# Experts in three chunks of 1024, 896 and 896 FF columns instead of six of 512 and 256

## What is computed

```python
def _moe(h, router_w, router_b, exp_gate, exp_up, exp_down):
    logits = (h @ router_w).astype(jnp.float32) + router_b.astype(jnp.float32)
    top_val, top_idx = lax.top_k(logits, TOP_K)
    wts = jax.nn.softmax(top_val, axis=-1)
    combine = jnp.sum(jax.nn.one_hot(top_idx, N_EXPERTS, dtype=jnp.float32) * wts[..., None], axis=-2)
    y = jnp.zeros_like(h)
    for e in range(N_EXPERTS):
        y = y + combine[..., e:e + 1] * _swiglu(h, exp_gate[e], exp_up[e], exp_down[e])
    return y

def _swiglu(h, w_gate, w_up, w_down):
    return (jax.nn.silu(h @ w_gate) * (h @ w_up)) @ w_down
```

## Time and profile before

| what | value |
| --- | --- |
| median of the runs | 1841.0 us |
| the profiled execution's own time | 1840.1 us |
| its span | 1838.2 us |
| TensorE busy | 1678.1 us, 91% |
| VectorE busy | 1247.9 us, 68% |
| ScalarE busy | 991.5 us, 54% |
| expert e0 (two tiles), first to last product | 912.5 to 1115.3 us of the span |
| experts e1 to e7 (one tile each) | 1115.3 to 1794.5 us |

### The profile page before, as it was taken

One profiled execution on the slowest core, in us unless ns is written; L12 is line 12 of the kernel. 1 busy time (PEld: TensorE's weight loads), 2 busy tenths in 40 slices (PEclk: granted clock), 3 DMA queues, 4 the chain that ended last, 5 costly groups with the idle time before them and its releaser, 6 DMA issues.

```text
span 1838.2 us, 20709 instructions
## 1 busy us (share of the span) xinstructions
PE 1678.1 (91%) x7867; PEld 1386.1 (75%) x7867; DVE 1247.9 (68%) x1518; ACT 991.5 (54%) x1322; POOL 88.7 (5%) x100
## 2 busy tenths in 40 slices
PE   6879989899999979998799998999999989999990
PEld 4767767788778758997687776878887878788780
DVE  5565356755453456766554456989988978998886
ACT  5753354343332342444443435778777767787770
POOL 0003300110000000000000000000000000000003
PEclk8989999999999989999799999999999999999995
DMA  8643235396454335655255557999999999999983
GB/s 310 203 138 116 69 130 165 99 316 247 140 177 138 106 100 168 199 183 183 96 183 180 163 186 269 373 363 376 378 375 370 376 333 356 370 379 375 378 320 114
DMA packets 205244, 436.59 MB, mean 238 GB/s; under 512 B 13391, under 2 KB 46778, under 8 KB 205114
## 3 DMA queue, kind: packets, MB, share of 16 engines
q1 hardware_dynamic: 195050, 398.20, 61.7%
q0 software_dynamic: 8368, 30.42, 4.9%
q10 hardware_dynamic: 1696, 6.29, 0.9%
HBM read 426.59 MB, written 20.86 MB: 243 GB/s over the span
## 4 chain that ended last, share of the span: by engine, by line
PE 73%; DVE 9%; DMA 7%; ACT 5%; issue 4%; POOL 1%; SPq 0%; ACTq 0%; DVEq 0%; POOLq 0%
PE ps L517 22%; PE ps L519 21%; PE ps L518 21%; DVE w_lo L436 5%; DMA raw<-in_exp_gate 3%; ACT w_hi L430 2%; DMA raw<-in_exp_up 2%; PE ps L1164 1%; PE ps L702 1%; PE ps L703 1%; ACT hf L1427 1%; DMA raw<-in_w_mod 1%; PE ps L931 1%; PE ps L730 1%; DVE prod_exp L2165 0%
## 5 line engine op out<-in xcount | busy, mean ns | idle before, releaser
L436 DVE TENSOR_TENSOR w_lo<-raw,w_hi 128x1024 fp32r<-128x1024 f32 (+1 forms) x760 | 893.5, 1217 | 247.3 <-ACT w_hi L430 240.6
L430 ACT CAST w_hi<-raw 128x1024 fp32r<-128x1024 f32 (+1 forms) x760 | 767.4, 1047 | 391.3 <-PE ps L519 269.7
L517 PE MATMUL ps<-w_hi,gT_hi 128*128 128x512 f32 x792 | 317.5, 401 | 19.3 <-DVE w_lo L436 9.2
L519 PE MATMUL ps<-w_hi,gT_lo 128*128 128x512 f32 x792 | 311.6, 393 | 0.0
L518 PE MATMUL ps<-w_lo,gT_hi 128*128 128x512 f32 x792 | 311.1, 393 | 0.0
L517 PE MATMUL ps<-w_hi,prodT_hi 128*128 128x512 f32 x528 | 211.5, 401 | 8.8 <-DVE prod_dense L2165 5.2
L519 PE MATMUL ps<-w_hi,prodT_lo 128*128 128x512 f32 x528 | 207.2, 392 | 0.0
L518 PE MATMUL ps<-w_lo,prodT_hi 128*128 128x512 f32 x528 | 206.8, 392 | 0.0
L517 PEld LDWEIGHTS ps<-w_hi,gT_hi 128*128 128x128 f32 x792 | 150.4, 190 | 53.6 <-issue 11.7
L519 PEld LDWEIGHTS ps<-w_hi,gT_lo 128*128 128x128 f32 x792 | 150.3, 190 | 32.4
L518 PEld LDWEIGHTS ps<-w_lo,gT_hi 128*128 128x128 f32 x792 | 150.5, 190 | 29.5
(11 more groups left out here) (357 smaller groups left out, 1843.7 us busy)
## 6 DMA issues: line engine op xcount, KB each, us to landing
raw<-in_exp_gate SPq DMA_DIRECT2D x176, 512.0 KB, 5.7
raw<-in_exp_up SPq DMA_DIRECT2D x176, 512.0 KB, 5.7
raw<-in_exp_down SPq DMA_DIRECT2D x176, 512.0 KB, 5.2
raw<-in_w_mod SPq DMA_DIRECT2D x96, 512.0 KB, 4.8
y_rows<-in_exp_up POOLq DMA_DIRECT2D x8, 1536.0 KB, 28.8
raw<-in_w_in_conv SPq DMA_DIRECT2D x24, 512.0 KB, 6.3
raw<-in_ffn_gate SPq DMA_DIRECT2D x22, 512.0 KB, 5.2
raw<-in_ffn_up SPq DMA_DIRECT2D x22, 512.0 KB, 5.9
```

The costliest lines, as they stand in the source:

```text
L430: nc.scalar.copy(w_hi[:, s, cols], raw[:, n % RAW, cols]).then_inc(sem("w_hi_ready"), 1)
L436: nc.vector.tensor_tensor(w_lo[:, s, cols], raw[:, n % RAW, cols], w_hi[:, s, cols].bitcast(F32), ALU.subtract).then_inc(sem("w_ready"), 1)
L517: nc.tensor.matmul(out, a[0], b[0], start=start, stop=False)
L519: return nc.tensor.matmul(out, a[1], b[0], start=False, stop=stop)
```

## The change

The experts get a list of their own, `EXP_ORDER`, of 36 units. Chunks are 1024, 896 and 896 FF columns. A gate or up unit holds two K blocks, each of the chunk's whole width, one DMA for each (rows of 4096 or 3584 bytes); a down unit holds two K blocks as before or, at the first of chunk 1 and the last of chunk 2, one. The list is gate 0, up 0, gate 1, down 0, up 1, gate 2, two units of down 1, up 2, two units of down 1, down 2, four units each where no count is given. With one tile, gate has banks 0 and 1, up 2 and 3, down 4 and 5. With more tiles, tile s has banks 2s and 2s + 1 for gate, up and down alike, and `banks_free` has TensorE wait, wherever the kind changes, until ScalarE or VectorE has read them; the down sums of an expert then go to `Y` in three parts (a copy and two additions) instead of two. Silu and the multiplication run once a chunk; the turning follows in four groups a chunk. The next expert's rows are asked for after unit 26 of 36 and turned after unit 33. The dense layer keeps its code.

```diff
+EXP_CHUNKS = [(0, 1024), (1024, 896), (1920, 896)]
+EXP_GROUPS = [(2, 2, 2, 2), (1, 2, 2, 2), (2, 2, 2, 1)]
+EXP_ORDER = [(kind, c, i) for kind, c, part in
+             (("gate", 0, range(4)), ("up", 0, range(4)), ("gate", 1, range(4)), ("down", 0, range(4)), ("up", 1, range(4)),
+              ("gate", 2, range(4)), ("down", 1, range(2)), ("up", 2, range(4)), ("down", 1, range(2, 4)),
+              ("down", 2, range(4))) for i in part]
+EXP_UNITS = len(EXP_ORDER)
+EXP_BLOCKS = FF // P
+GROUPS = 4 * len(EXP_CHUNKS)
+
+
+def exp_at(kind, c, i=3):
+    return EXP_ORDER.index((kind, c, i))
+
+
+TURN_AT = {exp_at("gate", c + 1, i): [4 * c + i] for c in (0, 1) for i in range(4)}
+TURN_AT |= {exp_at("down", 1, 2): [8, 9], exp_at("down", 1, 3): [10, 11]}
+ROWS_AT, TURN_ROWS_AT = exp_at("up", 2, 0), EXP_UNITS - 3
+
+
+def group_blocks(g):
+
+    sizes = EXP_GROUPS[g // 4]
+    return sum(sizes[:g % 4]), sizes[g % 4]
+
+
+def turns_at(u, tiles):
+
+    groups = TURN_AT.get(u, [])
+    if tiles > 1 and u == exp_at("down", 1, 2):
+        return []
+    return TURN_AT[u - 1] + groups if tiles > 1 and u == exp_at("down", 1, 3) else groups
...
+def flat_banks(ps, base, first, n):
+    return ps.rearrange("p b n -> p (b n)")[:, 512 * base + first:512 * base + first + n]
...
-        return ffn(w["exp_gate"][0][expert], w["exp_up"][0][expert], w["exp_down"][0][expert], n - U_MOE)
+        kind, c, i = EXP_ORDER[(n - U_MOE) % EXP_UNITS]
+        c0, width = EXP_CHUNKS[c]
+        src = w[f"exp_{kind}"][0][expert].rearrange("(k p) n -> p k n", p=P)
+        if kind != "down":
+            return [(1, src[:, 2 * i + j:2 * i + j + 1, c0:c0 + width]) for j in (0, 1)]
+        first, blocks = group_blocks(4 * c + i)
+        first += c0 // P
+        if blocks == 2:
+            return [(1, src[:, first + j:first + j + 1, :]) for j in (0, 1)]
+        return [(1, src[:, first:first + 1, 512 * j:512 * j + 512]) for j in (0, 1)]
...
-    name, key, _ = STREAM[n] if n < U_MOE else ("moe", None, 0)
+    if n >= U_MOE:
+        kind, c, i = EXP_ORDER[(n - U_MOE) % EXP_UNITS]
+        half = EXP_CHUNKS[c][1] if kind != "down" else D // 2 * group_blocks(4 * c + i)[1]
+        return slice(0, half), slice(half, 2 * half)
...
-        prod_exp = place("prod_exp", [P, 2, WIDE], F32, R_S)
-        prod_exp_more = place("prod_exp_more", [P, 1, WIDE], F32, R_COND_T, 1536)
+        prod_one = place("prod_one", [P, 1, D], F32, R_S)
+        prod_more = place("prod_more", [P, TILES, D], F32, R_P, 24 * KB)
+        oneT = [place(f"oneT_{x}", [P, EXP_BLOCKS, P], F32R, R_P, o * KB) for x, o in (("hi", 0), ("lo", 11))]
+        moreT = [place(f"moreT_{x}", [P, 8, T_ALL], F32R, R_P, o * KB) for x, o in (("hi", 0), ("lo", 12))]
...
+                def turn_prod(g):
+                    c, (first, n) = g // 4, group_blocks(g)
+                    prev = g - 1 if tiles == 3 else g - 2
+                    pe.wait_ge(sem("prod_ready"), weighed + 2 * c + (1 if first + n <= 4 else 2))
+                    if prev >= 0:
+                        pe.wait_ge(sem("pT_lo"), turned + prev + 1)
+                    for i in range(tiles):
+                        b, o = turn_place(tiles, g, i)
+                        for j in range(n):
+                            last = nc.tensor.transpose(ps[:, b, o + j * P:o + (j + 1) * P],
+                                                       prod[:, i, (first + j) * P:(first + j + 1) * P], ident)
+                    last.then_inc(sem("pT_turned"), 1)
+                def banks_free(u, kind, c, i):
+
+                    if tiles == 1:
+                        if u == 2 and e:
+                            pe.wait_ge(sem("y_staged"), tiles0)
+                        if c and i == 0 and kind == "gate":
+                            pe.wait_ge(sem("sg_ready"), gated + c)
+                        if c and i == 0 and kind == "up":
+                            pe.wait_ge(sem("prod_ready"), weighed + 2 * c)
+                    elif i == 0 or u == exp_at("down", 1, 2):
+                        if kind == "gate" and c:
+                            pe.wait_ge(sem("prod_ready"), weighed + 2 * c)
+                        elif kind == "up":
+                            pe.wait_ge(sem("sg_ready"), gated + c + 1)
+                            if c == 1:
+                                pe.wait_ge(sem("y_part"), parts0 + tiles)
+                            elif c == 2:
+                                pe.wait_ge(sem("y_mid"), parts0 + tiles)
+                        elif kind == "down" and c < 2:
+                            if i == 0:
+                                pe.wait_ge(sem("sg_ready"), gated + c + 2)
+                            else:
+                                pe.wait_ge(sem("prod_ready"), weighed + 6)
+
+                for u, (kind, c, i) in enumerate(EXP_ORDER):
+                    banks_free(u, kind, c, i)
+                    w = Weights(pe, expert_unit(u), e)
+                    if kind == "down":
+                        first, n = group_blocks(4 * c + i)
+                        pe.wait_ge(sem("pT_lo"), turned + 4 * c + i + 1)
+                        begins = (u, 0) == (exp_at("down", 0, 0), 0) if tiles == 1 else u in (
+                            exp_at("down", 0, 0), exp_at("down", 1, 0), exp_at("down", 1, 2))
+                        ends = u == EXP_UNITS - 1 if tiles == 1 else u in (exp_at("down", 0), exp_at("down", 1, 1), EXP_UNITS - 1)
...
+                    else:
+                        width = EXP_CHUNKS[c][1]
+                        for s in range(tiles):
+                            for j in (0, 1):
+                                for half, n in ((0, 512), (1, width - 512)):
+                                    cols = slice(j * width + half * 512, j * width + half * 512 + n)
+                                    last = product3(ps[:, bank_of(kind, s) + half, 0:n],
+                                                    [x[:, 2 * i + j, s * P:(s + 1) * P] for x in gT],
+                                                    (w.hi[:, cols], w.lo[:, cols]), i + j == 0, i == 3 and j == 1)
+                    w.used(last)
+                    for g in turns_at(u, tiles):
+                        turn_prod(g)
...
+                    if u == (TURN_ROWS_AT - 1 if tiles == 3 else ROWS_AT):
+                        if tiles == 1:
+                            pe.wait_ge(sem("sg_ready"), gated + 3)
+                        elif tiles == 3:
+                            pe.wait_ge(sem("pT_lo"), turned + GROUPS)
+                        next_rows(tiles0 + tiles, rows_bank)
+                    elif u == TURN_ROWS_AT:
                         pe.wait_ge(sem("rows_landed"), 16 * (e + 1))
-                        turn_rows(tiles0 + tiles, bank, g_rows)
-
-                def sums_out(phase):
-                    if tiles == 1:
-                        return
-                    if phase == 0:
-                        pe.wait_ge(sem("y_part"), parts0 + tiles)
-                    else:
-                        pe.wait_ge(sem("y_staged"), tiles0 + (tiles - 1))
-                ffn(gT, expert_unit, tiles, e, after_unit=between, after_phase=sums_out)
+                        turn_rows(tiles0 + tiles, rows_bank, g_rows)
...
+                for u, (kind, c, i) in enumerate(EXP_ORDER):
                     if u == COUNT_AT:
                         route.load(e + 1)
                     split_in_loop(act, act_split, u, e)
+                    if u == TURN_ROWS_AT + 1 and e < N_EXP - 1:
+                        gathered_hi(tiles0 + tiles, rows_bank, 0)
+                    for g in turns_at(u, tiles):
+                        hidden_hi(g)
+                    if kind == "gate" and i == 3:
+                        sums_at(u)
+                        if tiles > 1 and e + c == 0:
+                            act.wait_ge(sem("x_full"), 3 * TILES)
+                        for s in range(tiles):
+                            n = EXP_CHUNKS[c][1]
+                            last = nc.scalar.activation(prod[:, s, 0:n], flat_banks(ps, 2 * s, 0, n), ACT.Silu)
+                        last.then_inc(sem("sg_ready"), 1)
+                    if tiles > 1 and u == exp_at("down", 0):
+                        if e:
+                            act.wait_ge(sem("y_landed"), tiles0 * 16)
+                        sums_at(u)
+                        for s in range(tiles):
+                            nc.scalar.copy(Y[:, s, :], flat_banks(ps, 2 * s, 0, D)).then_inc(sem("y_part"), 1)
+                if tiles == 1:
+                    if e:
                         act.wait_ge(sem("y_landed"), tiles0 * 16)
...
+                    if kind == "up" and i == 3:
+                        dve.wait_ge(sem("sg_ready"), CHUNKS + len(EXP_CHUNKS) * e + c + 1)
+                        sums_at(u)
+                        for first, n in ((0, 512), (512, EXP_CHUNKS[c][1] - 512)):
+                            for s in range(tiles):
```

(60 more changed lines are left out.)

122 lines of the change are left out of this document (55 added, 67 removed).

## The result

The changed kernel takes 1890.6 us (median of 4 runs, 1884.2 to 1892.0); the kernel before took 1840.5 us beside it. The ratio is 1.0269, 95% interval 1.0253 to 1.0285: some 50 us lost, where the forecast was 30 and the range reached 53. The profiled execution took 1890.9 us, its span 1889.1.

What follows compares the result with a forecast made beforehand. Bound: TensorE, busy 94.2 us per single expert, with transfers and VectorE keeping up; e0 stops for PSUM reads. The profiled 1840.1 us plus 22 for e0 and 8 for the single experts made 1870 us; range 1845 to 1893.

Steps and rivals of the forecast that it cites:

- e0: Two-tile expert: nine TensorE stops at changes of kind, 23.6 us against 6.1; with clock and narrower matmuls +22 us.
- the clock: In the two-tile expert: half clock behind the five longest of nine stops, 1.25 us each, 6.3 against 2.5, +3.8 us.
- Columns: Single experts: 96 matmuls of 384 columns replace 72 of 512, +0.27 us an expert, +1.9 us in seven.
- Unit 26: Single experts: TensorE waits for this unit's splits by ScalarE and VectorE, 0.8 to 0.9 us each, +6 us in seven.
- The boundary: Between experts: the half unit at the end gives less cover for the next splits, 0.85 us more, +5 at six boundaries.
- Transfers: Single experts: longer gate and up rows take less DMA engine time and cure lateness, -5 us, bounds 0 and -7.6.
- The gain by long rows: DMA queue: 4 KB rows need 41.5 us of one engine per MB instead of 43.4 with 2 KB rows, 4.4% less.
- Rival 2: Weight ring feeds worse: less held, halves wait for both old halves; 1.5 us per short unit, 21 us, 1891 us; chance 0.13.
- rival 1: Single experts lose to transfers, which long rows cure, at most 19.8 us: 1844 us or 1833, not slower; chance 0.11.
- rival 4: Gate and up loads: long rows don't come about, packets stay at 2 KB, no -5, 1875 us; chance 0.08.
- rival 3: The ScalarE stall at e5 depends on where code lies: none gives 1861 us, two 1879; chance of two 0.10.

Runs made afterwards that it cites:

- e7: Not a run: the last of the eight experts, one tile; its stretch took 96.8 us in the kernel before.
- e5: Not a run: one of the seven one-tile experts; its stretch took 103.4 us in the kernel before, where ScalarE stood for 6.21 us.
- e6: Not a run: one of the seven one-tile experts; its stretch took 94.8 us in the kernel before.
- the first four experiments: Changed kernel with second halves at column 1024 (1882.2 us); that plus short gate/up rows (1884.3); with the one-block down unit second (1888.2); with half-size expert loads (1858.3).

## Why the prediction was right in sign and short by 20 us

**e0, right, with the clock still open.** Nine stops were forecast and nine came, 21.4 us for 23.6; the largest miss is the last, 1.3 for 2.0. The chain before down units is as put down, the turned pair first, then the Silu. ScalarE before the second of the stops shown above:

```profile
980.11 0.65 ACT L1847 CAST moreT_hi<-ps 128x256 fp32r<-128x256 f32 x2 [2.80 <-PE ps L1435]
980.64 1.75 ACT L1868 ACTIVATE prod_more<-ps 128x896 f32<-128x896 f32 x2
```

Two Silu of 896 took 1.75 us, for 1.7 assumed. The runs with e0 the old way give the whole as 28 and 23 us by medians. In the traces the old e0 takes 201 to 203 us (four traces); the new one takes 229.1 in the changed kernel's own trace and 221 to 225 in the five other runs that have it. So +26.3 is the upper end, and the forecast's +22 is the usual size. The open term was the clock. The forecast let five stops lose it (its own list has four of 2.9 and 3.0 us, not five), while in six traces of this e0 seven, three and four times two of the nine did (below), so that this term fits no single execution.

**Columns, nearly right.** Three steps of 384 columns in e4 (1505.65 to 1506.17 us on TensorE's timeline) take 0.52 us, 0.173 each, as in the earlier trace rows. Over all 96 of e4 in the run with four buffers the mean is 0.176, which makes 96 x 0.176 - 72 x 0.227 = 0.55 us an expert instead of 0.27, 4 in seven.

**Unit 26, mis-sized.** The wait is there in six of the seven experts, and in all with four buffers, but costs 0.35 us, not 0.8 to 0.9. e4, ScalarE, VectorE and TensorE, after the pair is turned at 1507.41:

```profile
1507.83 0.38 ACT L1847 CAST oneT_hi<-ps 128x256 fp32r<-128x256 f32 x1 [0.41 <-PE ps L1435]
1508.10 0.93 ACT L1868 ACTIVATE prod_one<-ps 128x896 f32<-128x896 f32 x1
1508.91 1.78 ACT L482 CAST w_hi<-raw 128x896 fp32r<-128x896 f32 x2
...
1509.88 2.10 DVE L488 TENSOR_TENSOR w_lo<-raw,w_hi 128x896 fp32r<-128x896 f32 x2 [0.68 <-ACT w_hi L482]
...
1512.12 0.47 PE L569 MATMUL ps<-w_hi,gT_hi 128*128 128x512 f32 x1 [0.20 <-DVE w_lo L488]
```

ScalarE begins 0.42 us after the turning, not 0.64 (two blocks are turned, where the earlier trace rows has four), and each instruction starts before the one ahead of it has ended: done after 3.3 us instead of 3.8. That is the difference: +2.5 us in seven experts, not +6.

**The boundary, right in kind.** With half the bytes or four buffers the stop before unit 2 is 0.76 to 0.82 us at all boundaries but the one into e7 and, with four buffers, the one into e3, 0.5 more than the 0.30 of before; 0.85 more was taken between bounds of 0 and 1.36, so +3 at six boundaries instead of +5. Moving the half unit from the end took it to 0.2 to 0.4 at three boundaries.

**Transfers, wrong: the step that failed.** The forecast gave them -5 us. A fourth buffer gives the changed kernel 31 us and the kernel before 8, so late weights cost +23 net (35 - 14 = 21 by half the bytes, 26.4 - 3.6 = 22.8 by the traces of the fourth buffer). Two things were wrong. The gain by long rows, 4.4% of a queue's time per MB, came from two stretches of 22 and 9 us with different kinds of weights in them; over 500 us it is 0.3% between the two kernels, 2.8% where the rows alone differ, and 2.3% with four buffers (0.942 x 16 x 500 / 176.68 = 42.7 us per MB in the changed kernel and 0.971 x 16 x 500 / 177.96 = 43.7 in the kernel before). And the term asked how long the transfers take, not when they may begin. Rival 2 had that: three buffers hold fewer bytes when units are narrower, and a half waits for both halves of a narrower old unit. It gave 1891 us, which is what came, at a chance of 0.13. That the number fits to 1 us is luck, as its 1.5 us a short unit was a guess. Its place was only partly right: it counted the two one-block units, whose places in the ring go to units 27 and 2, while most of the waits for weights are where units of 1024 take over from units of 896, at units 12 to 14 and 30 to 32. Of the 31 us the run with a fixed place puts 12 on the rule of the two halves; the rest goes only with a buffer more. The argument against rival 2, fewer engine microseconds, was the same 4.4%, and even a true gain in rate would not have let a load begin earlier; the row that spoke for it, TensorE's step and the transfers within 3% of each other, should have carried more weight.

**Rivals 1, 3 and 4 fell.** Singles with fewer late weights than before did not come about (rival 1); rows did become long (rival 4). The stop of ScalarE that the kernel before had at e5 has no counterpart among ScalarE's waits over e2 to e6, so what rival 3 would have given back is within the +28; two stops of VectorE, into e3 and e7, stand in its place.

The sum as measured, over the kernel before: e0 23 to 28, late weights 23 net, and 4 for the rest of the chunks (both with four buffers, e0 the old way): 50 to 55, against 50 by the median. The 4 is less than its parts, 2.5 for unit 26, 3 for the boundary and 4 for the columns, in part because the kernel before still has its stop at e5 with four buffers (TensorE idle for 5.07 us there) and the changed kernel has not.

## What to carry to other kernels

When a step of work is near the time of its transfers, ask first at what moment each load may be issued and which earlier instruction it waits for; a rate per byte says nothing about that, and narrower units in buffers of fixed size shorten the lead: a fourth buffer was worth 31 us here with units of 896 and 1024 columns and 8 us with full ones. Let pieces of different widths start at fixed places, so that a piece overlaps only its own predecessor. One more landing buffer tells, in one run, whether a stream is at its limit or just started late.

## What was not expected of the hardware

The granted clock behind the same stop differs from one execution to the next. Stretches of TensorE behind the first, second and third stop of e0 (PE busy, clock, DMA share, GB/s), in the changed kernel and in its run with four buffers, where e0 is the same code:

```profile
932.30:935.40 3.10, 3.10 (x14) 1.00 0.04 8
957.60:959.90 2.30, 2.30 (x10) 0.61 0.04 14
983.10:985.40 2.30, 2.30 (x7) 0.50 0.00 0
```

```profile
939.00:942.10 3.10, 3.10 (x14) 1.00 0.04 8
964.30:966.60 2.30, 2.30 (x9) 0.58 0.11 14
989.70:992.00 2.30, 2.30 (x12) 1.00 0.00 0
```

The third stop cost 2.53 us in both; behind it the clock was at the lower of its two levels, 0.50, in the one and 1.00 in the other. In the first execution matmuls run at half speed behind seven of the nine stops, in the second behind three, and that makes e0 229.1 or 223.0 us; in the changed kernel's runs of the first four experiments, with the same nine stops, it is two. The Trainium skill (TensorE: Matmul & The Clock Gate, HAM oscillation) has a loop of bursts and waits pay the throttled clock at every wait; its waits last 3 to 5 us. The prediction applied this to shorter stops, and by these rows a stop of 2 to 3 us pays it only sometimes.

VectorE can start late where nothing that the profile shows holds it. ScalarE and VectorE at unit 2 of e3, four buffers:

```profile
1334.79 2.00 ACT L496 CAST w_hi<-raw 128x1024 fp32r<-128x1024 f32 x2 [0.95 <-ACT Y L1898]
...
1338.12 2.36 DVE L503 TENSOR_TENSOR w_lo<-raw,w_hi 128x1024 fp32r<-128x1024 f32 x2 [3.74 <-ACT w_hi L496]
```

ScalarE's first half was done by 1335.8, yet VectorE began 2.3 us later, and TensorE waited 3.0 us. The changed kernel has such stops of 2.3 and 2.5 us into e3 and e7. They were absent with half the bytes in the changed kernel, yet with half the bytes the kernel before kept a stop of 4.2 us at e5. A late load of instructions fits, and the trace has one: in the 10 us from the first product of e3, and of e7, a DMA queue of the kind "instruction" moves three packets of 8 KB, where it moves two at e2, e4, e5 and e6. The changed kernel at e3, then at e4:

```profile
q14 instruction: 3, 0.02, 0.6%
```

```profile
q14 instruction: 2, 0.02, 0.4%
```

VectorE starts 1.55 and 1.51 us after the first of the three has landed, at e3 and at e7; at e2, e4 and e5 it starts before the first has. With half the bytes e3 and e7 have three packets as well. In the kernel before the queue has three at e5 too, and ScalarE ends its stop 1.28 us after one of them has landed. That the engines wait for these packets is argued from their order in time; no run takes the packets away.
